# Matmuls of 512 columns that take the high and the low part of the moving operand together, in a single-core transformer forward pass

## The chip, the core and the metric

The kernel runs on one NeuronCore of a Trainium2 chip. The metric is the device time of one execution in microseconds (us). The core has TensorE (PE, the matmul engine, which writes to PSUM), VectorE (DVE), ScalarE (ACT), GpSimd (POOL) and SyncE (SP, which issues the DMAs here). Each engine runs its own list of instructions in order; between engines there are only semaphores. PSUM has 8 banks (`b0` to `b7`), each of 128 partitions by 512 floats.

## The reference

The reference is a stack of sub-layers on x (256 tokens by 2048 features, f32): a mixer with a gated delta rule and block attention, cross attention to a memory of 256 tokens, a gated FFN with a short convolution and 5632 hidden features, a norm, a state-space (Mamba2) layer, a layer norm, a sliding-window attention layer and a last layer norm. Most of its arithmetic is in plain projections:

```python
def hybrid_mixer(x, ...):
    h = rmsnorm(x, norm_g)
    proj = h @ w_in
    ...
    return o @ w_out

def conv_ffn(x, norm_g, w_gate, w_up, conv_w, conv_b, w_down):
    h = rmsnorm(x, norm_g)
    gate = causal_dwconv(h @ w_gate, conv_w) + conv_b
    return (jax.nn.silu(gate) * (h @ w_up)) @ w_down
...
x = x + conv_ffn(...)
```

The state-space layer has `x @ w_in` (10240 columns) and `y @ w_out` likewise, and the last attention layer has its own two. The result is f32.

## The kernel before

Activations lie transposed, features on the partitions and the 256 tokens along the free dimension, so x is the tile `XT` of 16 blocks of 128 x 256. A **product** is one block of 128 output features of a projection: the sum over `kt` blocks of 128 input features (a **k-step** each) of a 128 x 128 weight block times a 128 x 256 activation block. The weights are the stationary operand, the activations the moving one.

To get near f32 precision at the speed of the type fp32r, every f32 operand is split in a high part (the value rounded to fp32r) and a low part (the rest): the weights in `WH` and `WL`, x in `XH` and `XL`, outputs of sub-layers in `OH` and `OL` (six further ones in `OX`, high and low side by side). A k-step is three matmuls of 256 columns into the same half bank, lines 766 to 768: `WH*XH`, `WH*XL`, `WL*XH`. The product of the two low parts is left out.

Weights come in chunks (at most 8 blocks of 128 columns, 512 KB) by DMA into five slots of `WR`. ACT writes the high part of a chunk to `WH` (L1236), DVE the difference to `WL` (L1647); both have four slots, and a slot is free when PE has used its chunk. `split` steps for a chunk stand three or four chunks ahead of its use, which is how far the splitting may run ahead of PE.

The order of all work is a list, `plan.steps`, made by `make_plan`. Each engine walks through the same list and emits its part of each step: `("half", ...)` are up to four k-steps of a product, `("evac", key)` is what empties its bank, and between halves `slot()` inserts a step of whatever small work is under way (the delta rule, attention, the state-space scan, all with f32 matmuls), `convA`/`gateA`/`cB` steps on a product (convolution taps, sigmoid or SiLU), and low parts. Products take the banks 0 to 2 in turn (`p["bank"] = self.big % 3`), and only the first 256 columns of one; only the products of `w_xo` go in pairs, one in each half of a bank (`"pair"`). A product may start when the one three before it has been emptied (`dve_ev.of(p["prior"])`).

Emptying is a DVE instruction that reads the bank, by kind: `conv` and `gate` (L1793, L1798: times the norm's factor `RB`), `plain` (L1810), `up` (L1853), `kv`, `xq`, `bkv`, `swg` (L1867), `swq` (L1873) and `res` (L1835: x plus the bank). ACT has no part in it but for one `Tanh` that reads the bank of a `swg` product (L1488).

There are 6,144 k-steps: `w_in` 56 products of 16 k-steps, `w_out` 32 of 8, `w_xkv` and `w_xq` 12 of 16, `w_xo` 16 of 4, `w_gate` and `w_up` 88 of 16, `w_down` 64 of 11, `a_w_in` 80 of 16, `a_w_out` 64 of 8, `kv_w` 4 and `b_w_in` 32 of 16, `b_w_out` 32 of 8.

## Time and profile before

| | |
|---|---|
| Runs | 2474.08 us (median of 3; 2471.7 to 2499.8) |
| Profiled execution, first to last instruction | 2471.0 us |
| PE busy | 2434.6 us (99%), 20,866 matmuls |
| PE weight load busy | 2376.3 us (96%) |
| DVE busy | 1727.8 us (70%) |
| ACT busy | 1220.4 us (49%) |
| POOL busy | 437.7 us (18%) |
| DMA, share of the 16 engines | 51% |
| Granted TensorE clock, mean | 0.998 |

The profile states no time of the execution beside the span; of the undisturbed runs one is 0.7 us above the span, the other 3.1 us. Busy times are unions: where instructions of an engine overlap, as matmuls do, they count once. So PE at 99% says that some matmul was in flight nearly always, not how fast they followed each other; that is read from their starts. The mean duration of a matmul (276 to 283 ns for 256 columns) is its latency; the distance of two starts is what it costs.

### The profile page before, as it was taken

To read this page: it belongs to the slowest core of one execution; us is meant where nothing else is said; L and a number is where in the kernel's file an instruction comes from. 1 tells how busy PE (TensorE), PEld (TensorE's weight loads), DVE (VectorE), ACT (ScalarE), POOL (GpSimd) and SP (SyncE) were. 2 spreads that over 40 slices of the span, in tenths; PEclk is the share of its full clock that TensorE was granted. 3 is DMA by queue.
4 is the path that set the end of the run, shared out by engine and by line. 5 is a ranking of instruction groups with operands and counts; after the bars stand their busy time and mean duration, and the time that the engine had idled before them with its cause. 6 is when DMAs were issued, how large, how long until landed. Compare 5 with 4: busy or idle time off the path is not lost.

```text
span 2471.0 us, 51530 instructions
## 1 busy us (share of the span) xinstructions
PE 2434.6 (99%) x20866; PEld 2376.3 (96%) x20866; DVE 1727.8 (70%) x2768; ACT 1220.4 (49%) x1918; POOL 437.7 (18%) x535
## 2 busy tenths in 40 slices
PE   7999999999999999999999999999999999999998
PEld 7999999999999999999999999999999999899998
DVE  6677646685666656665657877777787778777777
ACT  5434334554544444444444545444445554566554
POOL 1233310160200000000003201330101112511002
PEclk9999999999999999999999999999999999999999
DMA  6433335565455556556556654454454445444453
GB/s 220 158 124 120 127 126 180 189 200 171 155 196 193 193 176 212 197 176 212 195 174 190 195 167 157 161 179 156 156 189 153 158 158 183 151 154 144 149 163 118
DMA packets 124501, 418.34 MB, mean 169 GB/s; under 512 B 13796, under 2 KB 17644, under 8 KB 124012
## 3 DMA queue, kind: packets, MB, share of 16 engines
q1 hardware_dynamic: 124268, 415.06, 51.1%
q8 instruction: 167, 2.74, 0.4%
q14 instruction: 66, 0.54, 0.1%
HBM read 412.37 MB, written 3.68 MB: 168 GB/s over the span
## 4 chain that ended last, share of the span: by engine, by line
PE 93%; DVE 3%; POOL 2%; issue 1%; ACT 1%; DMA 0%; SPq 0%; ACTq 0%; POOLq 0%; DVEq 0%
PE b L766 27%; PE b L767 27%; PE b L768 27%; PE b L744 2%; PE b L1109 1%; DVE WL L1647 1%; PE b L887 1%; DVE t1s L1745 1%; PE b L900 1%; PE b L1120 1%; PE b L737 1%; POOL t1s L2547 0%; PE b L1175 0%; POOL ACC L2378 0%; PE b L1214 0%
## 5 line engine op out<-in xcount | busy, mean ns | idle before, releaser
L766 PE MATMUL b<-XH,WH 128*128 128x256 f32 x4224 | 1196.5, 283 | 18.2 <-DVE WL L1647 14.6
L768 PE MATMUL b<-XH,WL 128*128 128x256 f32 x4224 | 1173.5, 278 | 0.0
L767 PE MATMUL b<-XL,WH 128*128 128x256 f32 x4224 | 1173.4, 278 | 0.0
L1236 ACT ACTIVATE WH<-WR 128x1024 fp32r<-128x1024 f32 (+2 forms) x811 | 817.6, 1012 | 505.0 <-PE b L768 500.3
L1647 DVE TENSOR_TENSOR WL<-WR,WH 128x1024 fp32r<-128x1024 f32 (+2 forms) x811 | 984.5, 1223 | 14.9 <-ACT WH L1236 14.7
L766 PEld LDWEIGHTS b<-XH,WH 128*128 128x128 f32 x4224 | 795.7, 188 | 30.4 <-issue 14.2
L767 PEld LDWEIGHTS b<-XL,WH 128*128 128x128 f32 x4224 | 795.8, 188 | 3.0 <-issue 2.4
L768 PEld LDWEIGHTS b<-XH,WL 128*128 128x128 f32 x4224 | 797.0, 189 | 0.0
L766 PE MATMUL b<-OH,WH 128*128 128x256 f32 x1680 | 472.9, 282 | 2.9 <-DVE WL L1647 2.4
L768 PE MATMUL b<-OH,WL 128*128 128x256 f32 x1680 | 466.6, 278 | 0.0
L767 PE MATMUL b<-OL,WH 128*128 128x256 f32 x1680 | 466.5, 278 | 0.0
L766 PEld LDWEIGHTS b<-OH,WH 128*128 128x128 f32 x1680 | 316.6, 188 | 7.1 <-issue 6.1
L767 PEld LDWEIGHTS b<-OL,WH 128*128 128x128 f32 x1680 | 315.8, 188 | 1.6 <-issue 1.4
L768 PEld LDWEIGHTS b<-OH,WL 128*128 128x128 f32 x1680 | 316.1, 188 | 0.0
L1835 DVE TENSOR_TENSOR XT<-XT,b 128x256 f32<-128x256 f32 x192 | 80.6, 420 | 144.4 <-PE b L768 142.4
L1745 DVE SCALAR_TENSOR_TENSOR t1s<-cvs,par,t1s 128x256 f32<-128x256 f32 x304 | 150.2, 494 | 33.1 <-ACT t1s L1307 18.3
L1327 ACT ACTIVATE t1s<-t1s 128x256 f32<-128x256 f32 x156 | 64.8, 416 | 193.6 <-DVE t1s L1745 170.6
L2463 POOL TENSOR_TENSOR t2s<-t2s,RB 128x256 f32<-128x256 f32 x44 | 32.5, 739 | 559.6 <-DVE t2s L1773 559.6
L1793 DVE TENSOR_TENSOR cvs<-b,RB 128x256 f32<-128x256 f32 x116 | 48.8, 421 | 114.0 <-PE b L768 113.3
L2370 POOL TENSOR_TENSOR sms<-sms,con 128x2 f32<-128x2 f32 (+2 forms) x27 | 38.1, 1412 | 274.4 <-DVE sms L1967 98.0
L1773 DVE SCALAR_TENSOR_TENSOR t2s<-t1s 128x256 f32<-128x256 f32 x156 | 67.4, 432 | 8.3 <-ACT t1s L1327 8.3
L766 PE MATMUL b<-OX,WH 128*128 128x256 f32 x240 | 67.1, 280 | 0.0
(397 smaller groups left out, 2241.5 us busy)
## 6 DMA issues: line engine op xcount, KB each, us to landing
WR<-a_w_in SPq DMA_DIRECT2D x160, 512.0 KB, 3.7
WR<-w_in SPq DMA_DIRECT2D x112, 512.0 KB, 3.6
WR<-w_gate SPq DMA_DIRECT2D x88, 512.0 KB, 3.8
WR<-w_up SPq DMA_DIRECT2D x88, 512.0 KB, 4.2
WR<-a_w_out SPq DMA_DIRECT2D x64, 512.0 KB, 3.5
WR<-b_w_in SPq DMA_DIRECT2D x64, 512.0 KB, 3.5
WR<-w_down SPq DMA_DIRECT2D x64, 384.0 KB, 3.5
WR<-w_down SPq DMA_DIRECT2D x64, 320.0 KB, 2.9
```

Of the source, the lines that this page charges most:

```text
L744: last = pe.transpose(to[:, at:at + n], s, cc("ident", 0, n, n))
L766: mm(ps, WH[:, slot, at:at + P], xh, start=(k == 0), stop=False)
L767: mm(ps, WH[:, slot, at:at + P], xl, start=False, stop=False)
L768: m = mm(ps, WL[:, slot, at:at + P], xh, start=False, stop=(k == p["kt"] - 1))
L1236: act.activation(WH[:, s, 0:n], WR[:, r, 0:n], ACT.Copy).then_inc(*act_w.up(i))
L1327: act.activation(T1(2 + n % 2), T1(n % 2), ACT.Tanh, scale=0.5).then_inc(*act_cv.up("th", key))
L1647: dve.tensor_tensor(WL[:, s, 0:n], WR[:, r, 0:n], WH[:, s, 0:n].bitcast(F32), ALU.subtract).then_inc(*dve_w.up(i))
L1745: dve.scalar_tensor_tensor(y, b[:, j:j + S], pc(p["cw"], ci * K + j), y, ALU.mult, ALU.add).then_inc(*dve_cv.up("tap", key, j, also=("taps ...
L1773: dve.scalar_tensor_tensor(to, T1(2 + n % 2), 1.0, T1(n % 2), ALU.add, ALU.mult).then_inc(*dve_cv.up("end", key, also=("n", n)))
L1793: dve.tensor_tensor(cvs[:, p["c"] % 3, p["K"] - 1:p["K"] - 1 + S], ps, RB[:, :], ALU.mult).then_inc(*dve_ev.up(key))
L1835: dve.tensor_tensor(XT[:, m, :], XT[:, m, :], ps, ALU.add).then_inc(*dve_ev.up(key))
L2370: return pool.tensor_tensor(to[:, 0:n], columns[:, 0:n], cc("mhalf", 0, n), ALU.pow)
```

## The change

High and low parts of an activation now lie in one tile (`X2`, `O2`, of shape 128 x 2 x 16 x 256), so that one access pattern takes both. In every product but the `w_xo` pairs a k-step is two matmuls: `WH` times high and low part together, 512 columns into the whole bank, and `WL` times the high part, 256 columns into its second half (lines 777 and 778 of the new kernel). The first half of the bank then holds `WH*XH`, the second the two small terms, and somebody must add the halves. For `res` products DVE adds them to x one after the other. For all others ACT copies the second half to the place of the result (`low_half`, for two kinds with the bias), DVE adds the first half to it (`whole`), and then does its former operation on SBUF. Of a `swg` product the `Tanh` now reads the sum in SBUF, and the gating is a step of its own (`swa_gate`).

```diff
@@ -553,10 +555,9 @@
     WL = sb("WL", [P, HL, CK * P], F32R)
     XT = sb("XT", [P, 16, S])
     sb("apart", [P, 48])
-    XH = sb("XH", [P, 16, S], F32R)
-    XL = sb("XL", [P, 16, S], F32R)
-    OH = sb("OH", [P, 16, S], F32R)
-    OL = sb("OL", [P, 16, S], F32R)
+    X2 = sb("X2", [P, 2, 16, S], F32R)
+    O2 = sb("O2", [P, 2, 16, S], F32R)
+    XH, XL, OH, OL = X2[:, 0, :, :], X2[:, 1, :, :], O2[:, 0, :, :], O2[:, 1, :, :]
     with nc.sbuf_tensor("OX", [P, 12, S], F32R) as OX:
         pass
     t2x = sb("t2x", [P, 6, 512])
@@ -587,6 +588,10 @@
     def OS(i):
         return (OH[:, i, :], OL[:, i, :]) if i < 16 else (OX[:, 2 * (i - 16), :], OX[:, 2 * (i - 16) + 1, :])
 
+    def OS2(i):
+
+        return O2[:, :, i, :] if i < 16 else OX[:, 2 * (i - 16):2 * (i - 16) + 2, :]
+
     def pc(name, i=0, n=1):
         return par[:, POFF[name][0] + i:POFF[name][0] + i + n]
@@ -685,11 +690,15 @@
         return {"gdn": i, "att": i, "mem": MPLACE[i] if stage == "mem" else 0, "xat": 10 + i,
                 "up": (i // 11 % 2) * 11 + i % 11, "ssm": i % 16, "swa": i}[stage]
 
+    def wide(p):
+
+        return p["evac"] != "pair"
+
     def moving(key, k):
 
         src = plan.products[key]["src"]
         if isinstance(src, int):
-            return XH[:, k, :], XL[:, k, :], ("x", src, k)
+            return XH[:, k, :], XL[:, k, :], X2[:, :, k, :], ("x", src, k)
         name = key[0]
         if name == "wo":
             by = ("gdn", src[k]) if src[k] < 8 else ("att", src[k])
@@ -755,7 +764,7 @@
             w.wait_ge(*act_w.of(i))
             w.wait_ge(*dve_w.of(i))
             for k in range(k0, k1):
-                xh, xl, by = moving(key, k)
+                xh, xl, both, by = moving(key, k)
                 if by[0] == "x":
                     w.wait_ge(*act_x.of(by[1], k))
                     w.wait_ge(*(pool_x if by[1] == 4 and k % 2 else dve_x).of(by[1], k))
@@ -763,6 +772,11 @@
                     w.wait_ge(*act_os.of(*by))
                     w.wait_ge(*dve_os.of(*by))
                 at = (k - c0 + p["at"]) * P
+                if wide(p):
+                    full = banks[p["bank"]][:, :]
+                    mm(h2(full), WH[:, slot, at:at + P], both, start=(k == 0), stop=False)
+                    m = mm(full[:, S:2 * S], WL[:, slot, at:at + P], xh, start=False, stop=(k == p["kt"] - 1))
+                    continue
                 mm(ps, WH[:, slot, at:at + P], xh, start=(k == 0), stop=False)
                 mm(ps, WH[:, slot, at:at + P], xl, start=False, stop=False)
                 m = mm(ps, WL[:, slot, at:at + P], xh, start=False, stop=(k == p["kt"] - 1))
@@ -1470,8 +1484,66 @@
...
+        def low_half(key, p):
+
+            lo = banks[p["bank"]][:, half(1)]
+            kind, i, bias = p["evac"], key[1], None
+            w.wait_ge(*pe_prod.of(key))
+            if kind == "conv":
+                to = cvs[:, p["c"] % 3, p["K"] - 1:p["K"] - 1 + S]
+                if p["c"] > 2:
+                    w.wait_ge(*dve_cv.of("taps", conv_keys[p["c"] - 3]))
+            elif kind == "gate":
+                to = T1(p["n"] % 2)
+                if p["n"] > 1:
...
+            elif kind == "up":
+                to = T2(i % 4)[:, 0:S]
+                w.wait_ge(*pool_up.of(i))
...
+            if bias is None:
+                act.activation(to, lo, ACT.Copy).then_inc(*act_ev.up(key))
+            else:
+                act.activation(to, lo, ACT.Identity, bias=bias).then_inc(*act_ev.up(key))
+
         def evac(key):
             v = version(key)
+            p = plan.products[key]
+            if p["evac"] not in ("res", "pair"):
+                low_half(key, p)
             if v is not None:
                 residual_next(v, key)
             if key[:-1] in LAYER:
@@ -1783,19 +1854,27 @@
 
         def evac(key):
             p = plan.products[key]
-            ps = banks[p["bank"]][:, 0:S]
+            ps, lo = (banks[p["bank"]][:, half(j)] for j in range(2))
             kind, name = p["evac"], key[0]
+
+            def whole(to):
+                w.wait_ge(*act_ev.of(key))
+                dve.tensor_tensor(to, to, ps, ALU.add).then_inc(*dve_ev.up("sum", key))
+                w.wait_ge(*dve_ev.of("sum", key))
+                return to
+
             if key[:2] in (("so", 1), ("bo", 0)):
                 centred(*key)
             w.wait_ge(*pe_prod.of(key))
             if kind == "conv":
                 w.wait_ge(*dve_norm.of("rb", p["src"]))
-                dve.tensor_tensor(cvs[:, p["c"] % 3, p["K"] - 1:p["K"] - 1 + S], ps, RB[:, :], ALU.mult).then_inc(
-                    *dve_ev.up(key))
+                to = whole(cvs[:, p["c"] % 3, p["K"] - 1:p["K"] - 1 + S])
+                dve.tensor_tensor(to, to, RB[:, :], ALU.mult).then_inc(*dve_ev.up(key))
             elif kind == "gate":
                 if p["n"] > 1:
                     w.wait_ge(*dve_cv.of("n", p["n"] - 2))
-                dve.tensor_tensor(T1(p["n"] % 2), ps, RB[:, :], ALU.mult).then_inc(*dve_ev.up(key))
+                to = whole(T1(p["n"] % 2))
+                dve.tensor_tensor(to, to, RB[:, :], ALU.mult).then_inc(*dve_ev.up(key))
             elif kind == "plain":
                 pr = key[1]
                 if pr == 0:
@@ -1832,45 +1911,52 @@
...
-                dve.tensor_tensor(XT[:, m, :], XT[:, m, :], ps, ALU.add).then_inc(*dve_ev.up(key))
+                dve.tensor_tensor(XT[:, m, :], XT[:, m, :], ps, ALU.add).then_inc(*dve_ev.up("high", key))
+                w.wait_ge(*dve_ev.of("high", key))
+                dve.tensor_tensor(XT[:, m, :], XT[:, m, :], lo, ALU.add).then_inc(*dve_ev.up(key))
...
             elif kind == "up":
                 m = key[1]
                 gt = T2(m % 4)
                 w.wait_ge(*pool_up.of(m))
-                dve.scalar_tensor_tensor(gt[:, 0:S], ps, 0.5, gt[:, S:2 * S], ALU.mult, ALU.mult).then_inc(
-                    *dve_ev.up(key))
+                to = whole(gt[:, 0:S])
+                dve.scalar_tensor_tensor(to, to, 0.5, gt[:, S:2 * S], ALU.mult, ALU.mult).then_inc(*dve_ev.up(key))
...
             elif kind == "swq":
                 ti = key[1]
                 if ti > 1:
                     w.wait_ge(*pool_swa.of("q2", ti - 2))
                     w.wait_ge(*pe_swa.of("rope", ti - 2))
-                dve.tensor_scalar(T1(4 + ti % 2), ps, pc("q_b", ti), None, ALU.add).then_inc(*dve_ev.up(key))
+                w.wait_ge(*act_ev.of(key))
+                dve.tensor_tensor(T1(4 + ti % 2), T1(4 + ti % 2), ps, ALU.add).then_inc(*dve_ev.up(key))
...
@@ -280,6 +280,8 @@
         self.low_parts()
         if p["evac"] == "up":
             self.lows.append(("lowup", key[1]))
+        if p["evac"] == "swg":
+            self.lows.append(("swgate", key[1]))
         v = VERSION.get(key[:-1])
         if v is not None:
             self.lows.append(("xlow", v, key[-1]))
```

The order of the steps is the same. On PE, in the first products, the lists read so, before and then with the change (`X` is the tile `X2`):

```order
L768 MATMUL b<-XH,WL 128x256
L766 MATMUL b<-XH,WH 128x256
L767 MATMUL b<-XL,WH 128x256
L768 MATMUL b<-XH,WL 128x256
L766 MATMUL b<-XH,WH 128x256
...
L778 MATMUL b<-X,WL 128x256
L777 MATMUL b<-X,WH 128x512
L778 MATMUL b<-X,WL 128x256
L777 MATMUL b<-X,WH 128x512
```

Three matmuls and three weight loads a k-step have become two and two.

On DVE, in the FFN, one gate product (`cvs`) and one up product (`t2s`), before:

```order
L1647 TENSOR_TENSOR WL<-WR,WH 128x1024 [waits act_w] x2
L1793 TENSOR_TENSOR cvs<-b,RB 128x256 [waits pe_prod]
L1662 TENSOR_TENSOR OL<-t2s,OH 128x256 [waits act_os]
L1647 TENSOR_TENSOR WL<-WR,WH 128x1024 [waits act_w]
L1745 SCALAR_TENSOR_TENSOR t1s<-cvs,par,t1s 128x256 [waits pool_cv,act_cv]
L1745 SCALAR_TENSOR_TENSOR t1s<-cvs,par,t1s 128x256 [waits dve_cv]
L1647 TENSOR_TENSOR WL<-WR,WH 128x1024 [waits act_w]
L1773 SCALAR_TENSOR_TENSOR t2s<-t1s 128x256 [waits act_cv]
L1853 SCALAR_TENSOR_TENSOR t2s<-b,t2s 128x256 [waits pool_up,pe_prod]
```

And with the change:

```order
L1718 TENSOR_TENSOR WL<-WR,WH 128x1024 [waits act_w] x2
L1862 TENSOR_TENSOR cvs<-cvs,b 128x256 [waits act_ev,pe_prod]
L1872 TENSOR_TENSOR cvs<-cvs,RB 128x256 [waits dve_ev]
L1733 TENSOR_TENSOR O<-t2s,O 128x256 [waits act_os]
L1718 TENSOR_TENSOR WL<-WR,WH 128x1024 [waits act_w]
L1816 SCALAR_TENSOR_TENSOR t1s<-cvs,par,t1s 128x256 [waits pool_cv,act_cv]
L1816 SCALAR_TENSOR_TENSOR t1s<-cvs,par,t1s 128x256 [waits dve_cv]
L1718 TENSOR_TENSOR WL<-WR,WH 128x1024 [waits act_w]
L1844 SCALAR_TENSOR_TENSOR t2s<-t1s 128x256 [waits act_cv]
L1862 TENSOR_TENSOR t2s<-t2s,b 128x256 [waits act_ev,pool_up,pe_prod]
L1937 SCALAR_TENSOR_TENSOR t2s<-t2s 128x256 [waits dve_ev]
```

Each emptying is two instructions, and the first waits for ACT (`act_ev`) too. On ACT the same stretch had no instruction that waits for the end of a product to read it (the `pe_prod` of L1236 is that of a chunk four back). Now it reads:

```order
L1538 ACTIVATE cvs<-b 128x256 [waits pe_prod]
L1250 ACTIVATE WH<-WR 128x1024 [waits ld_raw4]
L1324 ACTIVATE t1s<-cvs,par 128x256 [waits dve_ev]
L1341 ACTIVATE t1s<-t1s 128x256 [waits dve_cv]
L1250 ACTIVATE WH<-WR 128x1024 [waits pe_prod,ld_raw0]
L1538 ACTIVATE t2s<-b 128x256 [waits pool_up,pe_prod]
L1283 ACTIVATE O<-t2s 128x256 [waits dve_ev]
```

L1538 is the new copy. In the whole program ACT gets 272 of them, DVE 444 instructions more (192 for `res` products, 236 second steps and 16 gatings of their own); POOL and SP do what they did.

## Rows read from the trace of the kernel before

**Rows 1.** The page: busy time and share of the span by engine.

```profile
PE 2434.6 (99%) x20866; PEld 2376.3 (96%) x20866; DVE 1727.8 (70%) x2768; ACT 1220.4 (49%) x1918; POOL 437.7 (18%) x535
```

**Rows 2.** The page: the chain that ended last, by engine and line.

```profile
PE 93%; DVE 3%; POOL 2%; issue 1%; ACT 1%; DMA 0%; SPq 0%; ACTq 0%; POOLq 0%; DVEq 0%
PE b L766 27%; PE b L767 27%; PE b L768 27%; PE b L744 2%; PE b L1109 1%; DVE WL L1647 1%; PE b L887 1%; DVE t1s L1745 1%; PE b L900 1%; PE b L1120 1%; PE b L737 1%; POOL t1s L2547 0%; PE b L1175 0%; POOL ACC L2378 0%; PE b L1214 0%
```

**Rows 3.** Timeline of PE: start us, length us, line, operands; FFN.

```profile
1000.04 0.28 PE L768 MATMUL b<-XH,WL 128*128 128x256 f32 x1
1000.15 0.28 PE L766 MATMUL b<-XH,WH 128*128 128x256 f32 x1
1000.26 0.28 PE L767 MATMUL b<-XL,WH 128*128 128x256 f32 x1
1000.38 0.28 PE L768 MATMUL b<-XH,WL 128*128 128x256 f32 x1
...
1005.48 0.28 PE L768 MATMUL b<-XH,WL 128*128 128x256 f32 x1
```

**Rows 4.** Timeline of PE, last projection.

```profile
2410.08 0.28 PE L767 MATMUL b<-OL,WH 128*128 128x256 f32 x1
...
2415.38 0.28 PE L767 MATMUL b<-OL,WH 128*128 128x256 f32 x1
```

**Rows 5.** Busy time by windows, PE alone: busy us (count), clock, DMA.

```profile
1393.00:1445.00 52.00, 52.00 (x444) 1.00 0.60 198
2391.00:2453.00 62.00, 62.00 (x529) 1.00 0.41 135
```

**Rows 6.** Timeline of PE, weights of 16 columns.

```profile
35.63 0.28 PE L784 MATMUL b<-XH,WH 128*16 128x256 f32 x1
35.74 0.28 PE L785 MATMUL b<-XL,WH 128*16 128x256 f32 x1
...
37.67 0.28 PE L784 MATMUL b<-XH,WH 128*16 128x256 f32 x1
```

**Rows 7.** Timeline of PE, plain f32 matmuls of 128 and 256 columns.

```profile
82.28 1.47 PE L737 MATMUL b<-con,sms 128*128 128x128 f32 x12
83.59 0.60 PE L744 MATMUL b<-con,t2s 128*128 128x128 f32 x4
...
2105.89 0.59 PE L1166 MATMUL b<-t1s,con 128*128 128x256 f32 x2
2106.32 0.59 PE L1165 MATMUL b<-XT,con 128*128 128x256 f32 x2
```

**Rows 8.** Durations (min/median/max ns) by line: plain f32, 256 and 512 columns.

```profile
L1166 PE MATMUL b<-t1s,con x16: 379/388/634, 2102.0 to 2462.1; 128*128 128x256 f32 x16
...
L1109 PE MATMUL b<-t2x,con x64: 591/592/697, 1453.9 to 2031.4; 128*128 128x512 f32 x64
```

**Rows 9.** Timeline of PE, first product, granted clock 1.2 GHz.

```profile
14.64 0.41 PE L768 MATMUL b<-XH,WL 128*128 128x256 f32 x1
...
18.48 0.41 PE L768 MATMUL b<-XH,WL 128*128 128x256 f32 x1
```

**Rows 10.** Windows: busy us (count) of PE, PEld, DVE, ACT, POOL; clock.

```profile
500.00:550.00 50.00, 49.11 (x429) 48.55 (x428) 45.77 (x59) 30.08 (x49) 40.67 (x39) 1.00 0.61 195
750.00:800.00 50.00, 50.00 (x443) 50.00 (x442) 33.04 (x49) 24.49 (x33) 3.88 (x10) 1.00 0.57 191
1350.00:1400.00 50.00, 49.44 (x430) 49.01 (x429) 43.24 (x62) 27.89 (x39) 16.98 (x19) 1.00 0.64 200
1400.00:1450.00 50.00, 50.00 (x428) 50.00 (x427) 42.84 (x71) 24.05 (x33) 6.34 (x12) 1.00 0.57 190
```

**Rows 11.** DVE and ACT by line: busy us, mean ns, idle before, releaser.

```profile
L1835 DVE TENSOR_TENSOR XT<-XT,b 128x256 f32<-128x256 f32 x192 | 80.6, 420 | 144.4 <-PE b L768 142.4
L1793 DVE TENSOR_TENSOR cvs<-b,RB 128x256 f32<-128x256 f32 x116 | 48.8, 421 | 114.0 <-PE b L768 113.3
L2241 DVE TENSOR_TENSOR t1s<-t1s 128x256 f32<-128x256 f32 x28 | 11.7, 419 | 0.0
L1488 ACT ACTIVATE t1s<-b 128x256 f32<-128x256 f32 x16 | 5.8, 365 | 3.0 <-PE b L768 3.0
```

**Rows 12.** Waits of PE between 20 and 2450 us: total, times, longest.

```profile
PE b L766 <- DVE WL L1647: 2.9, 5, 1.1
PE b L766 <- POOL XL L2603: 2.6, 4, 1.0
```

More of the change, by code:

```diff
@@ L1484, in evac @@
                 ti = key[1]
-                w.wait_ge(*pe_prod.of(key))
+                w.wait_ge(*dve_ev.of(key))
                 if ti:
-                    w.wait_ge(*dve_ev.of(("wg", ti - 1)))
-                act.activation(T1(8), banks[plan.products[key]["bank"]][:, 0:S], ACT.Tanh, scale=0.5).then_inc(
-                    *act_swa.up("th", ti))
+                    w.wait_ge(*dve_swa.of("g", ti - 1))
+                act.activation(T1(8), T1(ti % 4), ACT.Tanh, scale=0.5).then_inc(*act_swa.up("th", ti))
         def time(*what):
@@ L1808, in evac @@
                     w.wait_ge(*(pe_att.of("ns", pr - 2) if name == "mv" else pe_att.of("o", pr - 2)))
-                to = T2(SETS[pr % 2]["qkv".index(name[1])])[:, half(key[2])]
-                dve.tensor_tensor(to, ps, RB[:, :], ALU.mult).then_inc(*dve_ev.up(key))
+                to = whole(T2(SETS[pr % 2]["qkv".index(name[1])])[:, half(key[2])])
+                dve.tensor_tensor(to, to, RB[:, :], ALU.mult).then_inc(*dve_ev.up(key))
             elif kind == "res":
@@ L1839, in evac @@
                 if m < 4:
[L1840 removed]
+                    to = whole(KM[:, m, :])
                 else:
```

64 lines of the change are left out of this document (53 added, 11 removed).

## The prediction

> **What bounds the kernel now.** I read the page's busy times first, then the chain of waits, then PE's timeline, then the windows. PE is busy 99% and the chain is 93% PE, with 27% on each of the three matmul lines of a k-step [rows 1, 2]. Between 20 and 2450 us PE waits for nobody longer than 1.1 us at a time [rows 12]. So the time is PE's own instruction stream, and what counts is how far apart two matmuls start, since busy time counts latency too. In the FFN 16 k-steps take from 1000.04 to 1005.48 us: 340.0 ns a k-step, 113.3 ns a matmul [rows 3]. That is not the only pace. In the last projection 15 k-steps take 5.30 us: 353.3 ns, 117.8 ns a matmul [rows 4]. Two long stretches hold this slower pace throughout: 52 us with 444 matmuls and 62 us with 529, both 117.1 to 117.2 ns [rows 5]. From the starts in the whole timeline I count 5,042 intervals of 115 to 120 ns, nearly always after a run of small matmuls and until a later one; those of rows 4 are among the last. So some 1,680 k-steps go at the slow pace and 4,400 at the quick one.
>
> **What a matmul costs beyond its columns.** At the granted clock of 1.2 GHz six k-steps take 3.84 us, so 213.3 ns a matmul, 0.833 ns a column and nothing above [rows 9]. At 2.4 GHz that would be 106.7 ns for 256 columns; the quick pace lies 6.7 ns above. The weight load is not what makes these 6.7 ns: with weights of only 16 columns six k-steps take 2.04 us, again 340 ns [rows 6]. The change merges two of the three matmuls, so everything hangs on how the 6.7 ns scale. If they belong to a matmul, a k-step becomes 213.3 + 6.7 + 113.3 = 333.3 ns. If they belong to the columns (1/16 more time for each), it stays at 340. No fp32r matmul of 512 columns is in this trace. The nearest rows are the plain f32 matmuls, which take 0.83 ns a column: 12 of 128 columns start 109 ns apart, two of 256 columns take 430 ns, 215 each [rows 7]. 109 is 106.7 + 2.3, and 215 is 213.3 + 2: their surplus does not grow with columns. Nor does it up to 512 columns: the shortest durations there are 379 ns at 256 columns and 591 at 512 [rows 8], 212 ns for 256 columns more, the bare 0.83 ns a column. I therefore take a surplus for each matmul, which is where these rows point, and keep the other end for the range.
>
> The Trainium skill has a rule here (TensorE: Matmul & The Clock Gate, section "Wait — 56ns, not 53.3ns?"): warm matmuls start N/2.4 + about 2.5 ns apart, 215.7 ns at 512 columns, cold ones exactly N/1.2. The trace agrees in the cold stretch and for plain f32, and disagrees for fp32r at 256 columns (113.3 where the rule has 109.2). By the rule the merge would be worth 2.5 ns a k-step, 15 us in all, where my sum has more.
>
> **The sum.** Wide are all k-steps but the 64 of `w_xo`: 6,080.
> - Quick pace: 4,400 x 6.7 ns = −29 us. The other end is 0.
> - Slow pace: the surplus of 353.3 − 340 = 13.3 ns is on three matmuls. With two left, if each keeps its 4.4 ns, the k-step is 224.4 + 117.8 = 342.2, 11 ns less; if the slow pace comes from weight loads that find no time under 256 columns, the wide matmul loses it, as it covers a load twice over, and the k-step is 337.7 or less, 15.6 to 17 ns less. I take 14: 1,680 x 14 = −24 us (ends −18 and −29).
> - DVE gets 444 instructions of 0.42 us [rows 11], 186 us, and stands at 1,914 us of some 2,430, 79%. In most stretches this is covered: 33 us of 50 in the FFN with 9 products more at 0.42 us becomes 37 [rows 10]. In 1350 to 1400 and 1400 to 1450 it becomes 47, still under 50, with bursts that are not; I charge 3 us. In 500 to 550 (`w_out`, second part, products of 8 k-steps) there are 18 products: 45.8 + 18 x 0.42 = 53.4 us of work in 50 [rows 10], and PE must wait for `WL`: +4 us.
> - ACT gets 272 copies of about 0.37 us [rows 11], 100 us on 1,220: covered. What ACT and DVE add one after the other is delay. A product's result is there 0.37 + 0.42 us and two hand-overs later, about 0.9 us. DVE waits at each emptying for PE anyway (114 us before L1793 alone, 142 before L1835 [rows 11]), since it runs ahead; this lead is the cover, and if it goes PE waits for `WL` next. Where a chain through DVE and ACT must be back within one half product (four k-steps, 1.36 us), as in the delta rule, the 0.9 us do not always fit: +2 us.
> - Serial places (first norm with three products held back, three later norms, the last norm after the last product): 0.42 to 0.9 us each, +3 us.
> - DMAs: none added or moved; chunks are asked for 2% sooner at a 51% share, nothing. The bank a product takes is free after two further products, at least 5.3 us, against 0.9 us more for emptying: nothing. The gating of `swg` is used some slots later: nothing.
>
> Sum: −29 − 24 + 3 + 4 + 2 + 3 = −41 us. On the span of 2471.0 this is 2430; the median of the runs is 3.1 us above that span, and I carry that over: **2433 us**.
>
> **Rivals.**
> 1. *The surplus belongs to the columns.* For it: it is exactly 1/16 of the columns, and absent where columns come at half the rate (cold, plain f32), which is how a limit on the rate of reading 4-byte columns would look. Against it: nothing but the f32 rows. A wide matmul then takes 226.7 ns. Quick pace: 0. Slow pace: 226.7 + 117.8 = 344.5, 9 ns less, or 340, 13 less: −15 to −22 us. With the same +12 for DVE and ACT: −3 to −10, **2464 to 2471**, chance 0.32.
> 2. *The surplus of 6.7 ns is one of matmuls whose weight load has no slack, and a wide one keeps only the 2.3 ns of the f32 rows.* Against it: rows 6, with loads that have slack. A k-step is 215.6 + 113.3 = 328.9: 4,400 x 11.1 + 1,680 x 24.4 = −90, +12: **2396**, chance 0.15. The skill's rule above gives the same wide matmul (215.7 ns).
> 3. *DVE becomes the bound* (slower). Place: 1350 to 2100 us, where DVE is busiest with the state-space layer and some 135 products are emptied. Each costs 0.9 us more on a path that runs PE, ACT, DVE, and ACT stands in its own list behind the end of the product before it can split on. If ACT and DVE can't run ahead, about half of 135 x 0.9 = 122 us reaches PE, and the same in 500 to 550: +75 us, against at best −15 by rival 1: **2534**. It decides where DVE's work per 50 us goes past what PE needs; by rows 10 that is one window. Chance 0.07.
>
> A remainder of 0.03 is for something else.
>
> **How the numbers follow.** Forecast 0.43 (own range 2420 to 2450), rivals 0.32, 0.15, 0.07. The range 2392 to 2480 holds the forecast, rival 1 with a worse DVE term, and over half of rival 2: about 0.83. A measurement of this kernel tells about 2% from no change, 49 us, so faster means below 2425. That takes in rival 2 and a third of the forecast: 0.30. Slower is rival 3 and a bit of the remainder: 0.08. The rest, 0.62, is within 2%.
>
> **What would show it.** In the timeline of PE: 220 ns from a wide matmul to its narrow one (forecast), 227 (rival 1) or 216 (rival 2), and 113 from the narrow to the next wide one. The share of k-steps above 336 ns shows what became of the slow pace. PE's waits for `WL` should be near 10 us in all, most of them between 500 and 550 us; at 50 or more, rival 3 holds. DVE's busy time should be near 1,910 us, and the idle time of ACT before its new copy should name PE. I would be wrong on the whole if a wide matmul took more than 230 ns, for instance because its two halves lie 16 KB apart in SBUF, for which no row here has a price.

## The result, and the profile after

The changed kernel takes **2539.15 us** (median of 4; 2539.07 to 2539.30), the kernel before beside it 2485.68 us (median of 4; 2471.7 to 2499.8): a ratio of 1.0254 with a 95% interval of 1.0205 to 1.0302. It is slower. The forecast was 2433, the range ended at 2480. Executions of the kernel before fall in two groups, 2470 to 2476 and 2497 to 2504 us, both at the same granted clock, and two of the four lie in each; against the lower group, to which the profiled execution belongs, the ratio is 2539.15 / 2472.9 = 1.027. The span grew from 2471.0 to 2537.2 us, by 66.2.

The page of the changed kernel, lines that answer to [rows 1, 2]:

```profile
PE 2489.9 (98%) x14786; PEld 2142.7 (84%) x14786; DVE 1919.6 (76%) x3212; ACT 1310.8 (52%) x2190; POOL 431.7 (17%) x535
...
PE 85%; DVE 9%; POOL 2%; issue 2%; ACT 2%; DMA 0%; SPq 0%; POOLq 0%; DVEq 0%; ACTq 0%
PE b L777 49%; PE b L778 25%; DVE WL L1718 3%; DVE t1s L1816 2%; PE b L753 1%; PE b L1123 1%; PE b L901 1%; POOL ACC L2470 1%; PE b L914 1%; POOL t1s L2639 1%; POOL t1s L2495 0%; ACT WH L1250 0%; PE b L1134 0%; PE b L1189 0%; PE b L746 0%
```

PE has 6,080 matmuls fewer and is busy 55 us longer. The chain is still PE's, though DVE's share went from 3% to 9%, so both a slow PE and a late DVE are possible (the chain goes over to the releaser at every wait, however short it is). The timeline of PE decides between them. The changed kernel in the FFN (start us, length us, line, operands), against [rows 3]:

```profile
1000.14 0.28 PE L778 MATMUL b<-X,WL 128*128 128x256 f32 x1
1000.26 0.40 PE L777 MATMUL b<-X,WH 128*128 128x512 f32 x1
1000.49 0.28 PE L778 MATMUL b<-X,WL 128*128 128x256 f32 x1
1000.61 0.40 PE L777 MATMUL b<-X,WH 128*128 128x512 f32 x1
...
1005.44 0.28 PE L778 MATMUL b<-X,WL 128*128 128x256 f32 x1
1005.56 0.40 PE L777 MATMUL b<-X,WH 128*128 128x512 f32 x1
```

From 1000.14 to 1005.44 us are 15 k-steps: 353.3 ns each, where three matmuls had taken 340.0 in this place. From a wide matmul to its narrow one it is 0.23 to 0.24 us, from a narrow one to the next wide one 0.12. That is so nearly everywhere: of 6,080 intervals behind a wide matmul 5,613 are 235 or 236 ns, of 6,130 from a product matmul of 256 columns to the next product matmul 5,682 are 118 or 119. All intervals from one product matmul to the next together were 2139.1 us before and are 1457.8 + 739.6 = 2197.4 us now: **58.3 of the 66.2 us**. In the FFN alone, between the same two small matmuls of both traces, the changed kernel loses 28.2 us, and its 2,112 k-steps at 13.4 ns more would be 28.3. PE waits little for others; its waits in the changed kernel between 20 and 2500 us (total, times, longest), against [rows 12]:

```profile
PE b L777 <- DVE WL L1718: 4.5, 9, 1.1
PE b L777 <- POOL X L2695: 2.5, 4, 1.0
PE b L780 <- DVE WL L1718: 2.2, 2, 1.1
```

And the windows of the changed kernel, busy us (count) of PE, PEld, DVE, ACT, POOL, against [rows 10]:

```profile
500.00:550.00 50.00, 48.43 (x272) 41.41 (x271) 44.97 (x67) 26.39 (x43) 31.20 (x29) 1.00 0.62 193
750.00:800.00 50.00, 50.00 (x285) 43.42 (x284) 34.31 (x53) 26.25 (x41) 3.86 (x10) 1.00 0.58 188
1350.00:1400.00 50.00, 50.00 (x285) 43.45 (x284) 43.70 (x60) 24.29 (x36) 21.29 (x20) 1.00 0.62 181
1400.00:1450.00 50.00, 49.24 (x300) 43.25 (x299) 45.11 (x73) 27.42 (x40) 12.84 (x16) 1.00 0.60 192
```

In 750 to 800 us PE is without a gap, and of its 285 matmuls one or two lie across the edges: 141.5 k-steps of 353 ns; before it had 443 matmuls, 147 k-steps. DVE has room in each window, 45 us of 50 at most. The emptying itself looks as planned, by line in the changed kernel (busy us, mean ns, idle before, what ended it):

```profile
L1914 DVE TENSOR_TENSOR XT<-XT,b 128x256 f32<-128x256 f32 x192 | 80.4, 419 | 93.5 <-PE b L778 89.7
L1862 DVE TENSOR_TENSOR cvs<-cvs,b 128x256 f32<-128x256 f32 x116 | 48.5, 418 | 98.9 <-ACT cvs L1538 98.7
L1538 ACT ACTIVATE cvs<-b 128x256 f32<-128x256 f32 x116 | 44.1, 381 | 115.8 <-PE b L778 115.5
L1916 DVE TENSOR_TENSOR XT<-XT,b 128x256 f32<-128x256 f32 x192 | 80.8, 421 | 6.6
```

ACT still waits 116 us for PE ahead of the copy of a `cvs` product, and DVE 99 us for that copy ahead of its sum: both are early. So the time went into the distance of PE's matmuls, and two questions remain: is 235 + 118 the width, or something that came with it; and what did the emptying cost?

### The profile page after: what moved, and what is told of

It reads as the page before. It is cut to its first block, busy times and chain, and to the rows that moved or that the text cites. A ratio compares the mean times of both kernels' runs of the same rounds, so it can differ in the third digit from the quotient of the medians.

```text
span 2537.2 us, 39943 instructions
## 1 busy us (share of the span) xinstructions
PE 2489.9 (98%) x14786; PEld 2142.7 (84%) x14786; DVE 1919.6 (76%) x3212; ACT 1310.8 (52%) x2190; POOL 431.7 (17%) x535
## 4 chain that ended last, share of the span: by engine, by line
PE 85%; DVE 9%; POOL 2%; issue 2%; ACT 2%; DMA 0%; SPq 0%; POOLq 0%; DVEq 0%; ACTq 0%
PE b L777 49%; PE b L778 25%; DVE WL L1718 3%; DVE t1s L1816 2%; PE b L753 1%; PE b L1123 1%; PE b L901 1%; POOL ACC L2470 1%; PE b L914 1%; POOL t1s L2639 1%; POOL t1s L2495 0%; ACT WH L1250 0%; PE b L1134 0%; PE b L1189 0%; PE b L746 0%
## 5 line engine op out<-in xcount | busy, mean ns | idle before, releaser
L777 PE MATMUL b<-X,WH 128*128 128x512 f32 x4224 | 1525.0, 403 | 20.2 <-DVE WL L1718 16.5
L778 PE MATMUL b<-X,WL 128*128 128x256 f32 x4224 | 1187.6, 281 | 0.0
L777 PEld LDWEIGHTS b<-X,WH 128*128 128x128 f32 x4224 | 795.3, 188 | 219.8 <-issue 18.3
L1250 ACT ACTIVATE WH<-WR 128x1024 fp32r<-128x1024 f32 (+2 forms) x811 | 810.9, 1009 | 244.1 <-PE b L778 237.6
L778 PEld LDWEIGHTS b<-X,WL 128*128 128x128 f32 x4224 | 794.5, 188 | 3.0 <-issue 2.4
L777 PE MATMUL b<-O,WH 128*128 128x512 f32 x1616 | 580.5, 401 | 1.7 <-DVE WL L1718 1.6
L778 PE MATMUL b<-O,WL 128*128 128x256 f32 x1616 | 454.1, 281 | 0.0
L777 PEld LDWEIGHTS b<-O,WH 128*128 128x128 f32 x1616 | 303.9, 188 | 79.0 <-issue 6.0
L778 PEld LDWEIGHTS b<-O,WL 128*128 128x128 f32 x1616 | 303.5, 188 | 1.5 <-issue 1.4
L1914 DVE TENSOR_TENSOR XT<-XT,b 128x256 f32<-128x256 f32 x192 | 80.4, 419 | 93.5 <-PE b L778 89.7
L1538 ACT ACTIVATE cvs<-b 128x256 f32<-128x256 f32 x116 | 44.1, 381 | 115.8 <-PE b L778 115.5
L777 PE MATMUL b<-OX,WH 128*128 128x512 f32 x240 | 87.4, 400 | 0.0
L1916 DVE TENSOR_TENSOR XT<-XT,b 128x256 f32<-128x256 f32 x192 | 80.8, 421 | 6.6
L778 PE MATMUL b<-OX,WL 128*128 128x256 f32 x240 | 67.4, 281 | 0.0
```

The costliest lines, as they stand in the source:

```text
L777: mm(h2(full), WH[:, slot, at:at + P], both, start=(k == 0), stop=False)
L778: m = mm(full[:, S:2 * S], WL[:, slot, at:at + P], xh, start=False, stop=(k == p["kt"] - 1))
L1250: act.activation(WH[:, s, 0:n], WR[:, r, 0:n], ACT.Copy).then_inc(*act_w.up(i))
L1538: act.activation(to, lo, ACT.Copy).then_inc(*act_ev.up(key))
L1914: dve.tensor_tensor(XT[:, m, :], XT[:, m, :], ps, ALU.add).then_inc(*dve_ev.up("high", key))
L1916: dve.tensor_tensor(XT[:, m, :], XT[:, m, :], lo, ALU.add).then_inc(*dve_ev.up(key))
```

## Experiments

### What came with the width: tiles, banks, three matmuls again

The tiles alone, in the kernel before:

```diff
-    XH = sb("XH", [P, 16, S], F32R)
-    XL = sb("XL", [P, 16, S], F32R)
...
+    X2 = sb("X2", [P, 2, 16, S], F32R)
+    O2 = sb("O2", [P, 2, 16, S], F32R)
+    XH, XL, OH, OL = X2[:, 0, :, :], X2[:, 1, :, :], O2[:, 0, :, :], O2[:, 1, :, :]
```

> The kernel before, with only the tiles changed: high and low part of x in one tile, and of the sub-layers' outputs in another, three matmuls of 256 columns as before. Theory W: no change from before within 1%, 2472 to 2500 us, k-steps mostly 340 ns. Rival B (the place of the operands in SBUF sets the slow pace): k-steps of 353 ns throughout, about 2530 us.

Measured: 2471.89 us (2469.91 to 2476.51), ratio 1.000 (0.9991 to 1.001). The place of the operands costs matmuls of 256 columns nothing; for one of 512 that reads both blocks, see the streams below.

The changed kernel with its wide matmul cut into two of 256 columns, except in the first k-step of a product:

```diff
-                    mm(h2(full), WH[:, slot, at:at + P], both, start=(k == 0), stop=False)
+                    if k == 0:
+                        mm(h2(full), WH[:, slot, at:at + P], both, start=True, stop=False)
+                    else:
+                        mm(full[:, 0:S], WH[:, slot, at:at + P], xh, start=False, stop=False)
+                        mm(full[:, S:2 * S], WH[:, slot, at:at + P], xl, start=False, stop=False)
```

> The changed kernel with each matmul of 512 columns split again into two of 256 (high part into the first half of the bank, low part into the second) except in the first k-step of a product; tiles, copies and the two-step emptying stay as changed. Theory W (the 512-column matmul itself holds TensorE at its slow pace of 117.8 ns per 256 columns): most k-steps go back to 340 ns, and what is left over the kernel before is the price of the emptying, some 5 to 15 us: 2480 to 2500 us. Rival D (DVE and ACT in the emptying are what makes it slow): stays at 2525 to 2540 us. Rival B (writing two halves of a bank, or the common tile, sets the slow pace): k-steps stay at 353 ns and the time at 2530 to 2540 us.

Measured: 2530.26 us (2529.68 to 2531.43), ratio 1.0238 (1.0223 to 1.0253). Only 9 us came back, not the 40 to 60 of the first expectation. Its timeline of PE in the FFN shows why:

```profile
1000.11 0.28 PE L781 MATMUL b<-X,WH 128*128 128x256 f32 x1
1000.23 0.28 PE L782 MATMUL b<-X,WL 128*128 128x256 f32 x1
1000.35 0.28 PE L780 MATMUL b<-X,WH 128*128 128x256 f32 x1
1000.46 0.28 PE L781 MATMUL b<-X,WH 128*128 128x256 f32 x1
```

These are again three matmuls of 256 columns a k-step, but at the slow pace of [rows 4]: 79% of the intervals between them are 117 to 119 ns, in the kernel before 28%. Either the halves of the bank, the new emptying, or the single wide matmul at a product's start holds the slow pace. The next three kernels take these one at a time.

Emptying of the change behind the PE stream of before (ACT's copy is multiplied by 0, and the second addition to x too, so that the sums are those of before):

```diff
-            lo = banks[p["bank"]][:, half(1)]
+            lo = banks[p["bank"]][:, half(0)]
...
-                act.activation(to, lo, ACT.Copy).then_inc(*act_ev.up(key))
+                act.activation(to, lo, ACT.Copy, scale=0.0).then_inc(*act_ev.up(key))
```

> TensorE as in the kernel before (three matmuls of 256 columns into one half bank), but ACT and DVE empty the banks as in the changed kernel: the copy multiplies by 0 and DVE adds the product to it; for residual products DVE's second instruction adds 0 times the bank. So it has the 272 ACT and 444 DVE instructions of the change and none of its matmuls. Theory W (the changed kernel's 66 us are 58 of matmul pace and 8 of emptying): 2476 to 2486 us, k-steps mostly at 340 ns. Rival D (the traffic of DVE and ACT slows TensorE's reads, and so causes the 353 ns): 2525 to 2540 us.

Measured: 2490.63 us (2487.87 to 2491.27), ratio 1.0072 (1.0059 to 1.0086), so +18.7 us. That is above the one expectation and far below the other. The slow pace has its 28% as before, so the emptying does not set it. Where the time goes is seen in the windows of this kernel, columns as above:

```profile
500.00:550.00 50.00, 47.23 (x403) 46.33 (x402) 45.95 (x66) 26.76 (x44) 34.63 (x32) 1.00 0.59 188
...
750.00:800.00 50.00, 50.00 (x443) 50.00 (x442) 36.76 (x58) 27.27 (x41) 3.89 (x10) 1.00 0.59 200
...
1400.00:1450.00 50.00, 48.86 (x412) 47.82 (x411) 47.67 (x84) 28.32 (x45) 3.42 (x5) 1.00 0.54 179
```

In the kernel before they had 429, 443 and 428 matmuls [rows 10]: 26 are missing in 500 to 550 us (3 us), none in the FFN, 16 (2 us) in 1400 to 1450. The small matmuls come in the same order in both traces, so the delay can be read from them one by one: 4.0 us up to 480 us, 3.1 more up to 540, 2.9 up to 660, 0.6 in all the FFN, 1.3 up to 1450, and some 6 behind it, where stretches of either pace also fell otherwise.

The PE stream of before with one wide matmul at the start of each product, whose second half nobody reads:

```diff
-                mm(ps, WH[:, slot, at:at + P], xh, start=(k == 0), stop=False)
+                if k == 0 and p["evac"] != "pair":
+                    both = xh_both(key)
+                    mm(h2(banks[p["bank"]][:, :]), WH[:, slot, at:at + P], both, start=True, stop=False)
+                else:
+                    mm(ps, WH[:, slot, at:at + P], xh, start=(k == 0), stop=False)
```

> The kernel before (with high and low parts in common tiles), but the first of a product's matmuls is 512 columns wide, with the low part of x in the second half bank, which nobody reads. 120 ns more for each of some 500 products, 60 us, if nothing else changes: 2530 us, with most of the 256-column matmuls still at 113.3 ns. Theory M (a 512-column matmul leaves TensorE in the slow pace for what follows, as in the split kernel): most 256-column matmuls at 118 ns, 45 us more again, 2565 to 2585 us. Rival B (the split kernel was slow because its matmuls write two halves of a bank): 2530 us.

Measured: 2545.51 us (2544.54 to 2546.51), ratio 1.0296 (1.0282 to 1.0311). 464 wide matmuls cost 464 x (233.4 − 113.3) = 56 us by themselves (233.4 ns is measured below); the other 18 us are pace: the share of slow intervals rose from 28% to 51%. Both theories had a part of it, neither its size. The timeline of PE in the FFN shows why it is half (L774 is the wide matmul, L776 to L778 are narrow):

```profile
1000.07 0.28 PE L777 MATMUL b<-X,WH 128*128 128x256 f32 x1
...
1003.61 0.28 PE L777 MATMUL b<-X,WH 128*128 128x256 f32 x1
...
1003.84 0.39 PE L774 MATMUL b<-X,WH 128*128 128x512 f32 x1
1004.08 0.28 PE L777 MATMUL b<-X,WH 128*128 128x256 f32 x1
...
1009.30 0.28 PE L778 MATMUL b<-X,WL 128*128 128x256 f32 x1
1009.41 0.39 PE L774 MATMUL b<-X,WH 128*128 128x512 f32 x1
1009.64 0.28 PE L777 MATMUL b<-X,WH 128*128 128x256 f32 x1
```

Ahead of the first wide matmul 30 intervals take 3.54 us, 118 ns each; behind it 46 take 5.22 us, 113.5 each; behind the next it is 118 again. **Each wide matmul in the FFN of this kernel switches the pace of the product behind it:** over the 151 products between 673 and 1422 us the pace changed at every one of the 150 steps, with 233 or 234 ns from a wide matmul to the first narrow one where the quick pace followed, 225 or 226 where the slow one did. In the split kernel, with one matmul fewer behind each wide one in a product of 16 k-steps, the same 151 products are all slow, and it is 235 or 236 ns there (once 225).

Last, the split kernel with no wide matmul at all (in the first half of a bank the first k-step's product is a group of its own, so the sums of this kernel are not those of the others, and only its time is of use):

```diff
-                    mm(h2(full), WH[:, slot, at:at + P], both, start=(k == 0), stop=False)
+                    if k == 0:
+                        mm(full[:, 0:S], WH[:, slot, at:at + P], xh, start=True, stop=True)
+                        mm(full[:, S:2 * S], WH[:, slot, at:at + P], xl, start=True, stop=False)
```

> The split kernel (2530 us) without its last matmuls of 512 columns: in the first k-step of a product too, high and low part are two matmuls of 256 into the two halves of the bank. No matmul of 512 is left; the emptying is that of the change. If the one wide matmul a product kept TensorE in the slow pace: the pace goes back to mostly 113.3 ns, and the time to that of the emptying alone, 2488 to 2495 us. If writing two halves of a bank is what brings the slow pace: 2525 to 2535 us again.

Measured: 2492.73 us (2490.26 to 2519.82, 10 runs). The kernel before lay mostly in its upper group beside it, so the ratio of 1.000 (0.996 to 1.004) says little; against the four executions of the lower group beside it (median 2474.1) it is +19 us, what the emptying costs alone, and 31% of the intervals are slow. The halves of the bank have no part in it. **Removing one wide matmul a product from the split kernel gave back 37.5 us** (36.0 between the two profiled executions), of which its width in place of two narrow ones is 464 x (233.4 − 226.6) = 3. The wide matmuls do two things, then: they take 233 to 235 ns, and in the kernel they set the pace of the narrow ones behind them, which in the split kernel is nearly always the slow one.

### TensorE alone

Two kernels append streams to the end of the changed kernel, when no other engine works; each ran once. Ahead of each stream stand one or more f32 matmuls of one column:

```diff
+            for i in range(24):
+                mm(banks[1][:, :], wh[i], XH[:, i % 8:i % 8 + 2, :].rearrange("p a b -> p (a b)"), start=True, stop=True)
+            burst()
+            for i in range(24):
+                mm(h2(banks[2][:, :]), wh[i], X2[:, :, i % 8, :], start=True, stop=True)
```

> The changed kernel and behind its last result, on TensorE alone, four rounds of streams of 24 fp32r matmuls with nothing else running: 256 columns, 512 contiguous, 512 as two blocks of 256, 384, 128, and 256 alternating with 128; one to four small plain f32 matmuls ahead of each stream. Their results go nowhere. It measures the pace by itself. Theory W: 256 and shorter at 113.3 ns per 256 columns (0.4427 ns a column) at least in some rounds, 512 columns at 235 ns (0.460) in all rounds, contiguous or not. Rival, a fixed surplus: 512 columns at 220 ns. Rival, the layout: 235 ns as two blocks and 227 contiguous. The whole run is longer than the changed kernel's by the streams, 60 to 80 us.

Timeline of PE in this kernel, equal matmuls in one row; the first round has one small matmul ahead (two records), the second two:

```profile
2543.82 3.07 PE L1247 MATMUL b<-X,WH 128*128 128x256 f32 x24
2546.73 0.28 PE L1244 MATMUL b<-con 128*128 128x1 f32 x2
2546.87 5.84 PE L1250 MATMUL b<-X,WH 128*128 128x512 f32 x24
2552.55 0.28 PE L1244 MATMUL b<-con 128*128 128x1 f32 x2
2552.69 5.84 PE L1253 MATMUL b<-X,WH 128*128 128x512 f32 x24
...
2569.01 2.98 PE L1247 MATMUL b<-X,WH 128*128 128x256 f32 x24
...
2572.19 5.85 PE L1250 MATMUL b<-X,WH 128*128 128x512 f32 x24
```

L1250 reads 512 columns in one piece, L1253 the two blocks 16 KB apart: the same 5.84 us. Inside a stream the starts alternate between 231 and 236 ns, 233.4 on average (the first interval of each stream is 30 to 90 ns longer and left out here and below): 20 ns above the 213.3 of its columns, three times the surplus of 256 columns at the quick pace. So neither the fixed surplus of 220 ns nor the layout as a cause came true. The streams of 256 columns show both paces with nothing else running: 117.7 ns in the first round (2.91 us from its first start to the small matmul behind it), 113.3 in the other three (2.82). 384 columns take 174.7 ns in the first and third round and 173.3 in the other two, 128 take 111.8, and 256 and 128 in turn 228 to 229 a pair.

The second such kernel has pairs of wide and narrow, a single wide matmul ahead of narrow ones, and widths between:

> The changed kernel and behind its end four rounds of streams of fp32r matmuls on TensorE alone: 24 of 256 columns with the moving operand from high, low, high tile in turn; the same with results in first, second, second half of a bank; one of 512 and 23 of 256; 12 pairs of 512 and 256; 24 of 320; 24 of 448; 16 of 192. The first streams gave 113.3 or 117.7 ns at 256 columns, 173.5 at 384, 233.4 at 512, which fits 0.469 ns a column less 6.7 ns. If that line holds: 143.4 ns at 320, 203.4 at 448. If a pace per column holds (0.4427 or 0.460): 142 to 147 and 198 to 206. Theory M: after one matmul of 512 the 256s go at 118 ns in all rounds, and pairs of 512 and 256 take 353 ns. Rival B: alternating halves gives 118 ns in all rounds, one half 113.3 in some.

Timeline of PE there, the stream of pairs in the first round:

```profile
2554.33 0.28 PE L1259 MATMUL b<-X,WH 128*128 128x256 f32 x1
2554.45 0.39 PE L1258 MATMUL b<-X,WH 128*128 128x512 f32 x1
2554.68 0.28 PE L1259 MATMUL b<-X,WH 128*128 128x256 f32 x1
2554.80 0.39 PE L1258 MATMUL b<-X,WH 128*128 128x512 f32 x1
...
2556.43 0.28 PE L1259 MATMUL b<-X,WH 128*128 128x256 f32 x1
2556.55 0.40 PE L1258 MATMUL b<-X,WH 128*128 128x512 f32 x1
2556.78 0.28 PE L1259 MATMUL b<-X,WH 128*128 128x256 f32 x1
```

Behind the very first pair one to three take 344 to 347 ns (2554.45 to 2554.80 is 0.35), then they settle at 353.3 and stay, in all four rounds, with one small matmul ahead or two. **The changed kernel's k-step is reproduced by TensorE alone.** A single wide matmul, though, left the 23 narrow ones behind it at 113.3 ns in all rounds, so what it does to the pace in the kernel is not shown here. 448 columns took 202.3 ns, 320 took 146.7, 192 took 112. With two small matmuls ahead the halves of a bank in turn and one half alone both took 113.3; with one ahead the halves took 117.7 twice, one half 113.3 and 117.8.

### Wide ones together

```diff
-                    m = mm(full[:, S:2 * S], WL[:, slot, at:at + P], xh, start=False, stop=(k == p["kt"] - 1))
+                    later.append((full[:, S:2 * S], at, xh, k))
                     continue
...
+            for to, at, xh, k in later:
+                m = mm(to, WL[:, slot, at:at + P], xh, start=False, stop=(k == p["kt"] - 1))
```

> The changed kernel with another order inside a half: the four matmuls of 512 columns first, then the four of 256. If the slow pace comes from two lengths that alternate, the runs of equal length go at 226.7 and 113.3 ns and the time falls by 40 to 60 us, to 2480 to 2500 us. If it comes with the 512-column matmul as such, it stays at 235 ns each and the time at 2535 to 2545 us.

Measured: 2509.87 us (2509.53 to 2510.07), ratio 1.0155 (1.014 to 1.017). Timeline of PE in this kernel, four wide and four narrow in a row each:

```profile
1000.89 0.62 PE L785 MATMUL b<-X,WL 128*128 128x256 f32 x4
1001.35 1.09 PE L778 MATMUL b<-X,WH 128*128 128x512 f32 x4
1002.28 0.62 PE L785 MATMUL b<-X,WL 128*128 128x256 f32 x4
1002.74 1.09 PE L778 MATMUL b<-X,WH 128*128 128x512 f32 x4
```

Neither expectation came true: the time fell by 29 us. Four k-steps take 1.39 us here, 347 ns each, 6 less than in the changed kernel; over all k-steps the strict alternation costs 29 us, 4.8 ns each, since 32% of the narrow intervals stay slow in the new order too. The rest of the loss is width and emptying: 233.4 + 113.3 = 346.7 ns a k-step gives 4,400 x 6.7 − 1,680 x 6.6 = +18 us against the kernel before, and with the 18.7 of the emptying +37, where +38.5 was measured.

### What a product's emptying costs by kind

The kernel before with a second DVE instruction on `res` products only, times 0:

```diff
+                w.wait_ge(*dve_ev.of("high", key))
+                dve.scalar_tensor_tensor(XT[:, m, :], ps, 0.0, XT[:, m, :], ALU.mult, ALU.add).then_inc(*dve_ev.up(key))
```

> The kernel before, with a second DVE instruction for residual products alone (0 times the bank added to x): 192 DVE instructions of 0.42 us, no ACT copies and nothing on the other products. The whole emptying cost 18.7 us with TensorE as before. If that is mostly the second part of the output projection between 500 and 550 us and its surroundings, where DVE has 46 us of work in 50: 2478 to 2484 us. If it is the hand-over from ACT to DVE in the other products: 2472 to 2476 us.

Measured: 2480.27 us (2476.44 to 2482.13, 10 runs). Its ratio, 0.9931 (0.990 to 0.996), is again to a kernel before that was mostly in its upper group. Against the lower group beside it (median 2474.1) it is +6 us, between the two profiled executions +8.5. So of 18.7 us some 6 to 8 are the second additions to x, and some 11 to 12 the 272 hand-overs through ACT; this split rests on the two groups being kept apart. Read from the small matmuls as above, this kernel has lost 0.7 us up to 480 us, where the one with the whole emptying has lost 4.0, and 3.2 from 480 to 540, where the other lost 3.1. So 3.3 us of the hand-overs through ACT fall in the first mixer's delta rule and attention, and the burst in the second part of `w_out` is DVE's additions alone.

### What sets the pace of the kernel before

Small f32 matmuls ahead of eleven gate products, one of the state-space layer and one of the last projection; first two, then one:

```diff
+            if k0 == 0 and (key[0] == "fg" and key[1] % 4 == 1 or key in (("bo", 0, 4), ("sc", 0))):
+                for _ in range(2):
+                    mm(banks[p["bank"]][:, S:S + 1], U, ones[:, 0:1], start=True, stop=True)
```

> The kernel before, with two plain f32 matmuls of one column (into a half bank that nobody reads) ahead of 13 products: 11 of the FFN, one of the state-space layer, one of the last projection. In the streams, two such matmuls ahead were followed by the quick pace each time, a single one mostly by the slow pace. If that holds here, the last projection and the FFN run at 340 ns a k-step; each pair of small matmuls costs about 0.35 us (4.5 us in all) and 4 to 5 us are won back: 2466 to 2476 us. If the pace after them is a matter of chance: up to 25 us slower in some executions.

> The same with one small f32 matmul ahead of the 13 products instead of two. If a single one sets the slow pace, the 600 us of the FFN go at 353 ns a k-step: 24 us more, 2490 to 2500 us, which would also explain the executions of the kernel before at 2497 and 2500 us. If it does not: 2470 to 2478 us.

Measured: with two 2476.02 us (2475.5 to 2478.5), ratio 0.9997 (0.9947 to 1.0047); with one 2488.57 us (2488.19 to 2491.47), ratio 1.0048 (0.9998 to 1.0098). Of the seven executions of the kernel before beside them one lay in the upper group; against the other six (median 2473.4) it is +2.7 and +15.2 us. Windows of the kernel with one small matmul:

```profile
750.00:800.00 50.00, 50.00 (x430) 50.00 (x429) 30.31 (x45) 23.56 (x31) 3.09 (x8) 1.00 0.59 190
900.00:950.00 50.00, 50.00 (x444) 50.00 (x443) 28.17 (x44) 21.64 (x29) 0.77 (x2) 1.00 0.57 180
```

Both windows are plain FFN, 50.00 us busy. In 900 to 950 the matmuls go at the quick pace, in 750 to 800 at the slow one for 40 of 50 us, though DVE and ACT are less busy there than in the same window of the kernel before, at the quick pace (33.04 and 24.49 us, [rows 10]). In the whole timeline of the FFN each run between two small matmuls (384 to 1,368 long) is of one pace from its first few matmuls to its end, and the eleven runs are slow and quick **strictly in turn**, slow first. In all, 46% of the intervals are slow against 28%, which is the 15 us. With two small matmuls ahead all eleven runs are quick. The kernel before has one unbroken run of 6,324 matmuls there, from 662 to 1380 us, quick in the profiled execution.

With two small matmuls ahead of three products only (second gate product, first of the state-space layer, fifth of the last projection):

> The kernel before with two f32 matmuls of one column ahead of three products only: the second gate product of the FFN, the first product of the state-space layer and the fifth of the last projection. In the kernel before one unbroken run of 6,295 matmuls, from 662 to 1380 us, went at the quick pace; at the slow one it would take 6,295 x 4.4 ns = 28 us more, about the distance between the two groups in which its executions fall (2470 to 2476 and 2497 to 2503). Theory (the pace is chosen by what stands right ahead of a run and kept to its end; the upper group is this run at the slow pace): no execution here above 2480, whatever the kernel before does beside it; the time is 2472 + 3 x 0.5 for the added matmuls - 900 x 4.4 ns for the two long slow stretches at 1393 and 2391 us = 2467 to 2472. Rival (the two groups are a state of the chip or of the memory, not of this run): executions of this kernel fall in two groups 26 us apart in the same share as those of the kernel before.

Measured: 2471.84 us (2470.77 to 2472.49, 11 runs), ratio 0.9999 (0.9989 to 1.0008). Its windows, against [rows 5]:

```profile
1393.00:1445.00 52.00, 52.00 (x460) 51.81 (x459) 46.57 (x77) 25.99 (x36) 3.42 (x5) 1.00 0.60 201
2391.00:2453.00 62.00, 62.00 (x546) 61.53 (x542) 45.83 (x66) 25.62 (x35) 14.11 (x15) 1.00 0.42 137
```

460 matmuls for 444, 546 for 529: both long slow stretches became quick, as expected, worth 4 us (other small matmuls, which the kernel before has too, stand between the added ones and these stretches, so the effect is not a direct one); the small matmuls and other stretches that fell into the slow pace (two near 1803 and 2050 us, 968 matmuls) took it back. All 15 executions of the kernel before beside it lay in the lower group too, so it doesn't tell what the upper group is. The runs above say one thing on it: on the chip where 15 of 19 executions of the kernel before lay in the upper group, the kernel with the second addition had none of 10 some 26 us above the rest, and the split kernel without wide matmuls one of 10 (2519.82 us). So it is not a state of the chip that slows every kernel. No version beat the kernel before.

## Why the prediction was wrong

**The step that failed** is the one under "What a matmul costs beyond its columns": "I therefore take a surplus for each matmul". It priced the wide matmul at 220 ns; it takes 235 in the kernel, 233.4 in a stream of its own. The rows behind it were of plain f32 matmuls [rows 7, 8], whose columns come at half the rate (0.83 ns each, against 0.44 for fp32r at the quick pace), and a surplus read there did not carry over to fp32r. The rule of the Trainium skill (TensorE: Matmul & The Clock Gate, section "Wait — 56ns, not 53.3ns?") has 215.7 ns; the streams here disagree by 18 ns, the kernel by 19. For plain f32, too, the trace agrees with that rule less than the prediction says: only the surplus of about 2.5 ns is alike, as the rule has 55.6 ns at 128 columns and rows 7 have 109. The Trainium skill (TensorE: Matmul & The Clock Gate, section "Back-to-back issue gap") gives about 131 ns for a sustained matmul of 512 columns; the stream here took 233.4.

**Quick pace, −29 us:** its 4,400 k-steps went from 340.0 to 353.4 ns, 4,400 x 13.4 = +59. **Slow pace, −24 us:** 353.3 before, 353.4 after, 0. Together +59, against 58.3 in the intervals; some 4 of these 58.3 are intervals longer than either pace, behind waits, so the agreement is a little better than it should be. The two terms missed by 112 us. The price of the wide matmul is some 4,400 x 15 = 66 of them; 4,400 x 4.7 = 21 are the narrow matmul behind it, which became slower, and 24 are the gain in the slow pace, which did not come.

**Emptying, +12 us** (3 + 4 + 2 + 3): 18.7 us alone, with PE as before, some 11 of them through ACT. The hand-over chains, charged at 2 us, are the undersized term: up to 480 us alone they cost 4.0 − 0.7 = 3.3. The second part of `w_out`, charged at 4, cost 3. In the changed kernel the intervals that touch a small matmul grew by 8.2 us, and with the 4 above that is 12: the sum came out as forecast, but not because each term was right; probably its slower PE covers part of the 18.7, which is argued and not shown. The busy time forecast for DVE, 1,910 us, came to 1919.6.

**Rival 1**, a surplus by the column, had the direction (226.7 ns) and not the size: 512 columns carry 20 ns, 256 carry 6.7 or 11. **Rival 2** was wrong on the same rows as the forecast. **Rival 3** came out near the time, 2534, by a mechanism that did not happen: PE's waits for `WL` between 20 and 2500 us are 4.5 + 2.2 = 6.7 us, against 2.9 [rows 12]. That its time was near is luck.

The condition "a wide matmul took more than 230 ns" came true, but not for the cause named beside it: the 16 KB between the halves cost nothing. And the slow pace, which I treated as a property of places in the program, is one into which a stream can fall, and which strict alternation of 512 and 256 columns held in every stream and nearly everywhere in the changed kernel. That the narrow matmul itself could become slower, 113 to 118 ns, was in no case of mine.

What the prediction had right: PE's stream is the bound, the weight load is not, and DVE at 76% is no obstacle.

## What to carry to other kernels

The price of a matmul type at a width is not read from another type: when a change rests on the fixed part of an instruction's cost and the trace has no such instruction, the range must reach to a surplus that grows faster than the width. Fusing two matmuls into a wider one can gain only what is fixed in them, here at most 6.7 ns of 113, and it brought a second emptying step with it, 19 us by itself. Read distances of starts, not busy time: 29% fewer matmuls left PE at 98% and made it slower.
